# A delta rule whose decay rows are read from HBM with a broadcast, and whose decay factors form during the step ahead

## What is computed

```
g = cumsum(g)                                      # per head, over the chunk
decay = exp(g[:, None] - g[None, :])               # where i >= j, else 0
L = strict_lower((beta*k) @ k.T * decay);  A = L + I
u, w = solve(A, v*beta), solve(A, k*beta*exp(g))
qk = (q @ k.T) * decay
v_new = u - w @ S
o = (q*exp(g)) @ S + qk @ v_new
S = S*exp(g_last) + (k*exp(g_last - g)).T @ v_new
```

## Time and profile before

| | us |
|---|---|
| median of 3 runs | 3170.73 |
| range of the runs | 3170.51 to 3170.89 |
| the profiled execution, its own time | 3172.82 |
| its span | 3171.0 |
| TensorE busy | 3027.9 |
| DVE, ACT, POOL busy | 1636.5, 963.3, 959.6 |
| mean granted TensorE clock | 0.987 of full |

### The profile page before, as it was taken

One profiled execution on the slowest core, in us unless ns is written; L12 is line 12 of the kernel. 1 busy time (PEld: TensorE's weight loads), 2 busy tenths in 40 slices (PEclk: granted clock), 3 DMA queues, 4 the chain that ended last, 5 costly groups with the idle time before them and its releaser, 6 DMA issues.

```text
span 3171.0 us, 45836 instructions
## 1 busy us (share of the span) xinstructions
PE 3027.9 (95%) x19048; PEld 2834.2 (89%) x19048; DVE 1636.5 (52%) x2465; ACT 963.3 (30%) x1661; POOL 959.6 (30%) x497
## 2 busy tenths in 40 slices
PE   7999999999988887899999999999999999999997
PEld 6999999999878885699899999989999887798996
DVE  6556666884555555466767776212212348531223
ACT  3212212443522226532121223212112337532222
POOL 0333333323321210233333333232222222344442
PEclk9999999999999998999999999999999999999998
DMA  5434444224300012233433432121211210122221
GB/s 198 143 118 135 126 138 133 99 69 139 110 19 1 1 41 65 72 102 125 134 124 128 146 121 86 61 67 60 61 61 60 78 47 2 61 94 93 94 92 62
DMA packets 124444, 282.63 MB, mean 89 GB/s; under 512 B 40014, under 2 KB 57166, under 8 KB 123982
## 3 DMA queue, kind: packets, MB, share of 16 engines
q1 hardware_dynamic: 121358, 272.24, 26.9%
q10 hardware_dynamic: 2880, 7.45, 0.6%
HBM read 268.08 MB, written 15.08 MB: 89 GB/s over the span
## 4 chain that ended last, share of the span: by engine, by line
PE 86%; DVE 6%; ACT 4%; issue 2%; POOL 1%; DMA 1%; ACTq 0%; SPq 0%; DVEq 0%; POOLq 0%
PE psum L1658 76%; PE psum L1796 2%; PE psum L1788 2%; PE psum L1895 1%; DVE o_acc L1483 1%; PE psum L1883 1%; ACT prob_o L1175 1%; DVE prob_o L1595 1%; PE psum L1876 1%; PE psum L1836 1%; PE psum L1802 0%; ACT cacc L1022 0%; ACT dE L1141 0%; DVE ada_w L1376 0%; PE psum L1825 0%
## 5 line engine op out<-in xcount | busy, mean ns | idle before, releaser
L829 POOL TENSOR_TENSOR wl<-raw,wh 128x1024 fp32r<-128x1024 f32 (+1 forms) x326 | 831.4, 2550 | 1712.2 <-ACT wh L907 1711.0
L1658 PE MATMUL psum<-uh,wh 128*128 128x256 f32 (+5 forms) x2704 | 661.7, 326 | 21.2 <-DVE ul L1230 11.2
L1658 PE MATMUL psum<-uh,wl 128*128 128x256 f32 (+5 forms) x2704 | 660.7, 326 | 0.0
L1658 PE MATMUL psum<-ul,wh 128*128 128x256 f32 (+5 forms) x2704 | 660.7, 325 | 0.0
L1658 PE MATMUL psum<-ah,wh 128*128 128x386 f32 (+4 forms) x2192 | 595.7, 344 | 5.5 <-POOL wl L829 4.4
L1658 PE MATMUL psum<-ah,wl 128*128 128x386 f32 (+4 forms) x2192 | 591.2, 342 | 0.0
L1658 PE MATMUL psum<-al,wh 128*128 128x386 f32 (+4 forms) x2192 | 588.8, 341 | 0.0
L1658 PEld LDWEIGHTS psum<-uh,wh 128*128 128x128 f32 (+1 forms) x2704 | 452.3, 190 | 45.3 <-issue 23.8
L1376 DVE SCALAR_TENSOR_TENSOR ada_product<-ada_w,cb 128x1024 f32<-128x1024 f32 x256 | 478.2, 1868 | 5.1
L1658 PEld LDWEIGHTS psum<-uh,wl 128*128 128x128 f32 (+1 forms) x2704 | 452.5, 189 | 19.8
L1658 PEld LDWEIGHTS psum<-ul,wh 128*128 128x128 f32 (+1 forms) x2704 | 451.5, 190 | 19.9
(11 more groups left out here) (211 smaller groups left out, 2515.1 us busy)
## 6 DMA issues: line engine op xcount, KB each, us to landing
raw<-in_w SPq DMA_DIRECT2D x264, 512.0 KB, 3.6
ada_w<-in_ada_w SPq DMA_DIRECT2D x128, 512.0 KB, 3.9
raw<-in_w SPq DMA_DIRECT2D x64, 448.0 KB, 3.7
spill<-cacc ACTq DMA_DIRECT2D x16, 384.0 KB, 2.4
scale_w<-in_scale_w SPq DMA_DIRECT2D x8, 512.0 KB, 14.4
ada_start<-in_ada_w SPq DMA_DIRECT2D x8, 512.0 KB, 14.6
ada_w<-bias_final SPq DMA_DIRECT2D x16, 256.0 KB, 3.1
h<-in_xT SPq DMA_DIRECT2D x8, 384.0 KB, 14.3
```

The source lines that it names most:

```text
L829: nc.gpsimd.tensor_tensor(wl[n % SPLIT_SLOTS][:, 0:k * w], raw[n % RAW_SLOTS][:, 0:k * w], wh[n % SPLIT_SLOTS][:, 0:k * w].bitcast(f32), A ...
L1658: ins = nc.tensor.matmul(pair[0:w, lo:hi], wt[n % SPLIT_SLOTS][:, k * w:(k + 1) * w], xt[:, k, cols], start=first, stop=last)
```

## The change

A new item `("rows",)` follows the last projection. TensorE transposes the sums `gc` of all 48 combinations of chunk, direction and head into 48 rows of 128, DVE copies them to SBUF (into `dQS[0]`), and SP stores them in HBM (`rows_hbm`). For the steps 1 to 5 SP then reads the four rows of a direction straight into `dE`, each into all 128 partitions: for step 1 as soon as they are stored, for step st + 2 after `dnU` of step st. Those steps have no products of the gates any more. DVE's subtraction now reads `dE` in SBUF and stands in the step ahead, behind `dnN` of level 4 (direction 0) and of level 5 (direction 1); ACT's two functions stand behind `dnY` of the same levels. POOL's queue is as it was. Step 0 is formed as before. Branches for norms that are not late, which this program never takes, are deleted as well, so line numbers move.

```diff
+    s += [("rows",)]
...
+            def load_rows(st, d):
+                first = 8 * SCAN[d][st] + 4 * d
+                sp.dma_start(dE[2 * (st % 2) + d][:, :, :], rows_hbm[first:first + 4, :].unsqueeze(0).to_broadcast([P, 4, P])) \
+                    .then_inc(rows_loaded[d], 16)
...
+                if x == ("rows",):
+                    sp.wait_ge(rows_ready, 1)
+                    sp.dma_start(rows_hbm, gc_rows[0:STEPS * 8, :]).then_inc(rows_stored, 16)
+                    sp.wait_ge(rows_stored, 16)
+                    sp.wait_ge(product_done, number[("proj", 0, "nv", 3)] + 1)
+                    for d in range(2):
+                        load_rows(1, d)
+                if x[0] == "dnU" and x[1] + 2 < STEPS:
+                    sp.wait_ge(product_done, number[x] + 1)
+                    sp.wait_ge(dif_done, group(x) + 3)
+                    load_rows(x[1] + 2, x[2])
...
+            def decay_factor(st, d):                       # ACT
+                n, b = 2 * st + d, 2 * (st % 2) + d
+                act.wait_ge(dif_done, n + 1)
+                nc.scalar.activation(dE[b][:, :, :], dE[b][:, :, :], ACT.Abs).then_inc(abs_done, 1)
+                act.wait_ge(abs_done, n + 1)
+                nc.scalar.activation(dE[b][:, :, :], dE[b][:, :, :], ACT.Exp, scale=-1.0).then_inc(decay_ready, 1)
...
-                elif x[0] == "dnA":
...
+                elif x[0] == "dnA" and x[1] == 0:
+                    decay_factor(0, x[2])
...
+                if x[0] == "dnY" and x[2] == 1 and x[1] < LAST and x[3] in (4, 5):
+                    decay_factor(x[1] + 1, x[3] - 4)
...
+            def decay_difference(st, d):                   # DVE
+                b = 2 * (st % 2) + d
+                dve.wait_ge(rows_loaded[d], 16 * st)
+                nc.vector.tensor_tensor(dE[b][:, :, :], dE[b][:, :, :], per_head(gc, SCAN[d][st], d), ALU.subtract).then_inc(dif_done, 1)
...
+                elif x[0] == "rows":                       # DVE
+                    dve.wait_ge(product_done, i + 1)
+                    nc.vector.tensor_copy(gc_rows[0:STEPS * 8, :], banks_of(x)[0:STEPS * 8, 0:P]).then_inc(rows_ready, 1)
...
+                if x[0] == "dnN" and x[2] == 1 and x[1] < LAST and x[3] in (4, 5):
+                    decay_difference(x[1] + 1, x[3] - 4)
...
+                elif x[0] == "rows":                       # PE
+                    pe.wait_ge(cum_scaled, 1)
+                    nc.tensor.transpose(pair[0:STEPS * 8, 0:P], gc[:, :, :].rearrange("p t c -> p (t c)"), ident[:, :]) \
+                        .then_inc(product_done, 1)
...
-                    for hd in range(4):
+                    for hd in range(0 if x[1] else 4):
                         c = 4 * d + hd
                         nc.tensor.matmul(pair4(pair, 0)[:, hd, :], decay[:, tile, c:c + 1].to_broadcast([P, P]), masks[:, U[d], :],
```

More of the change, by code:

```diff
@@ L224, in build @@
     late_no = {m: i for i, m in enumerate(LATE_NORMS)}
-    early_no = {x[1]: i for i, x in enumerate([x for x in norm_items if x[1] not in late_no])}
     norm_of = lambda x: 3 * x[1] + 2 * x[2] if x[0] in ("gate", "up", "down") else 3 * x[1] + 1
@@ L340, in build @@
         scratch = nc.dram_tensor("spill", (16, P, T), f32, kind="Internal").ap()
+        gc_rows = dQS[0][:, 0, :]
+        rows_hbm = nc.dram_tensor("rows_hbm", (STEPS * 8, P), f32, kind="Internal").ap()
         toeplitz = nc.dram_tensor("toeplitz", (16, NA_HEADS, 15, 48), f32, kind="Internal").ap()
@@ L362, in build @@
         squared, sq_summed, std_ready, rstd_ready = sem("squared"), sem("sq_summed"), sem("std_ready"), sem("rstd_ready")
-        normed, u_hi, u_lo = sem("normed"), sem("u_hi"), [sem(f"u_lo{i}") for i in range(2)]
         silu_done, glu_done, a_hi, a_lo = sem("silu_done"), sem("glu_done"), sem("a_hi"), sem("a_lo")
@@ L376, in build @@
         z_loaded = [sem(f"z_loaded{j}") for j in range(len(zt))]
+        rows_ready, rows_stored, rows_loaded = sem("rows_ready"), sem("rows_stored"), [sem(f"rows_loaded{d}") for d in range(2)]
         masks_loaded, table_made, bias_made, nv_loaded, nqk_loaded, m8_loaded, rope_loaded = (sem(n) for n in
@@ L421, in released @@
                 return [(cum_read, 2)]
+            if kind == "rows":
+                return [(rows_ready, 1)]
             if kind == "dnT":
                 return [(at_ready, n), (qk_ready, n)]
-            return [({"norm": std_ready, "gate": silu_done, "up": glu_done, "l2": l2_std,
+            return [({"norm": std_ready, "l2": l2_std,
                       "cum": cum_read, "dnA": lmat_done, "dnN": n_ready, "dnY": y_ready, "dnX": x_ready, "dnV": kd_ready,
@@ L629, in build @@
         dny_split_at = {("S", j): j for j in range(STEPS)}
[L631 to L643, removed]
         def mod_terms(x, *terms):
@@ L1091, in _ @@
                             finish_product(y)
[L1092 to L1099, removed]
                 elif x in scaled_no:
@@ L1104, in _ @@
                         gates()
[L1105 to L1116, removed]
                 elif x[0] == "l2":
@@ L1352, in a_matrix @@
                 d, n, tile, b = x[2], group(x), SCAN[x[2]][x[1]], work(x)
+                dve.wait_ge(product_done, number[x] + 1)
                 dve.wait_ge(em_ready, n + 1)
@@ L1433, in _ @@
                             finish_product(y)
[L1434 to L1456, removed]
+                    for k in range(KD if x == final else 0):
+                        if k >= 2:
+                            dve.wait_ge(out_stored[k % 2], 16 * (k // 2))
+                        nc.vector.scalar_tensor_tensor(out=sq[k % 2][:, 0:last], in0=h[:, k, 0:last],
+                                                       scalar=norm_g[:, 3 * DEPTH, k:k + 1], in1=rstd[:, u_cols(0, last)],
+                                                       op0=ALU.mult, op1=ALU.mult).then_inc(out_ready, 1)
                 elif x in scaled_no:
@@ L1461, in _ @@
                         gates()
[L1462 to L1473, removed]
                 elif x[0] == "abt":
@@ L1495, in _ @@
                                                    op0=ALU.mult, op1=ALU.mult).then_inc(cum_read, 1)
+                elif x[0] == "rows":
+                    dve.wait_ge(product_done, i + 1)
+                    nc.vector.tensor_copy(gc_rows[0:STEPS * 8, :], banks_of(x)[0:STEPS * 8, 0:P]).then_inc(rows_ready, 1)
                 elif x[0] == "dnA":
                     d, n, tile, b = x[2], group(x), SCAN[x[2]][x[1]], work(x)
-                    dve.wait_ge(product_done, i + 1)
-                    nc.vector.tensor_tensor(dE[b][:, :, :], pair4(banks_of(x), 0), per_head(gc, tile, d),
-                                            ALU.subtract).then_inc(dif_done, 1)
+                    if x[1] == 0:
+                        dve.wait_ge(product_done, i + 1)
+                        nc.vector.tensor_tensor(dE[b][:, :, :], pair4(banks_of(x), 0), per_head(gc, tile, d),
+                                                ALU.subtract).then_inc(dif_done, 1)
                     if d == 1:
@@ L1728, in _ @@
                         fresh_norm[0] = m
-                        if m in late_no:
-                            pe.wait_ge(shift_lo, KD + late_no[m])
-                            ready = lambda k: pe.wait_ge(late_lo, KD * late_no[m] + k + 1)
-                        else:
-                            ready = lambda k: pe.wait_ge(u_lo[k % 2], KD // 2 * early_no[m] + k // 2 + 1)
+                        pe.wait_ge(shift_lo, KD + late_no[m])
+                        ready = lambda k: pe.wait_ge(late_lo, KD * late_no[m] + k + 1)
                     if x[0] == "down" and x[4] == 0:
```

1 line of the change is left out of this document (removed).

## The result

The changed kernel takes 3148.57 us (median of 4 runs, 3146.39 to 3152.17), the kernel before 3170.62 (4 runs, 3164.04 to 3170.89): a ratio of 0.9936, 95% interval 0.9920 to 0.9952. Forecast were 3149.5 us and a range of 3145 to 3158. The profiled execution took 3149.65, its span is 3147.9, 23.1 less than before.

A forecast was written before the change was run, and what follows sets the result against it. TensorE was taken as the bound, with the decay factor's relay in the transitions. 14.8 + 5.4 - 0.3 + 1.3 = 21.2 off 3172.82 gives 3151.6; the profile stands 2.1 above the median, so 3149.5; range 3145 to 3158.

The forecast's parts named there:

- What bounds the kernel: TensorE, busy 3027.9 of 3171.0 us; its waits are above all in the delta rule's five transitions between steps.
- The relay: In each transition, the decay factor's way through DVE, ACT, ACT, POOL ahead of `a_matrix`; said to go.
- the rival in which a new wait eats half: DVE and POOL meet again, each transition gives only TensorE's 1.79 us: 9.0 in all, 3161.7 us; chance 0.10.
- What goes: Transitions lose 16 TensorE instructions (1.79 us) and the relay: 3.7 us each, 14.8 for four; POOL becomes the bound.
- The first transition: From step 0 to 1, with `dnU` in place of `dnK`: 5.4 us earlier.
- What is added: Subtractions (0.69), ACT's functions and POOL's masks inside the levels fit in idle time: cost nothing.
- The rival of disturbed levels: POOL's 20 moved masks each hold up DVE by 1.12 us, 22.4 come back: 3171.9 us, no change; chance 0.05.
- The start: TensorE's first products of `dnA` wait for DVE's copy of the rows: 0.3 us lost, bounds 0 and 1.6.
- The transfer: A 256 KB load of rows takes 4.1 us by the nearest row, within more than 15 us of slack: costs nothing.
- The rival of late rows: Loads of rows take 48 us, some 28 too late, in four steps 112: 3261 us, slower; chance 0.05.
- The clock: Two transitions lose 1.29 us each to clock falls after TensorE's 1.85 us hole; one fall saved, 1.3 us.
- TensorE's busy time: Sign of being right: TensorE is 8.9 us less busy.

The follow-up runs named there:

- The experiment without the early part: Changed kernel with subtraction, absolute value and exponential back at dnA of their own step, products of the gates still gone: 3170.88 us, ratio 1.0001 to the kernel before.
- its own experiment: Changed kernel with POOL's four masks of dnT reordered, A of both directions first, then the two transposes: 3144.98 us, ratio 0.9924 to the kernel before.
- the experiment with other banks: Changed kernel with the transposed rows in other PSUM banks, those of the item cum: 3150.75 us, ratio 0.9931 to the kernel before.

## Why the prediction was right, point by point

- *What bounds the kernel.* Right. The relay and TensorE's products run side by side in a transition. The experiment without the early part gives the time of before, with the products gone. The rival in which a new wait eats half falls: POOL's three masks stayed at 1.27 or 1.28 us and the additions took 0.69 and 0.83, so the two engines hardly met.
- *What goes.* Right in every link that sets the length of the transition. Forecast from `dnV`: POOL's mask of A of direction 1 ends after 11.85, measured 11.81; DVE's second mask after 13.15, measured 13.12; `dnX` after 15.85, measured 15.93. Off the path, level 1 of direction 0 started after 9.99 in place of 10.25. The first transition: the second mask after 11.35, measured 11.34; 5.4 shorter forecast, 5.58 measured at `dnX` (18.82 to 13.24). Without the clock the five came to 20.2 forecast; measured 22.77 less the two falls before (1.30 and 1.31) is 20.16. That POOL is the new bound was confirmed by its own experiment. There, I expected 1.2 us in the four transitions and 1.4 in the first, and got 1.07 and 1.08. No row of that run shows TensorE waiting in front of level 1, so what bounds the transition next is open.
- *What is added.* Right as to nothing, with one detail off. The subtraction took 0.78 on average in place of 0.69: five of the ten run beside POOL's mask and take 0.88. They have two inputs in SBUF, the masks and copies of the levels have one input in PSUM and stayed at 0.69. That is what the Trainium skill says on the page "SBUF — State Buffer", section "SBUF: two separate sides", and the trace agrees. The rival of disturbed levels falls: no mask or copy of the levels took over 0.69. The row that the prediction holds against it doesn't bear on it, though: DVE's mask at 1044.62 starts after POOL's work ends at 1044.54. The mask before it does, at 1043.65, with 0.69 as well.
- *The start.* 0.3 forecast, 0.17 measured (45.12 to 45.29, and the experiment with other banks gives it back).
- *The transfer.* 4.1 from the nearest row, 3.2 measured. The rival of late rows falls: nothing waited. By the Trainium skill, page "DMA: Bandwidth & Descriptors", section "Anatomy of one DMA — SWDGE (gpsimd) path", it would be 2.6, an estimate. That section is about transfers that GpSimd issues, and these are issued by SP; the measurement decides.
- *The clock.* The sum is right by luck, the picture only by half. I took one fall saved of two, 1.3 us, as the middle between none and both. Both transitions lost theirs (2.61), and a new one came in level 4 of step 5 (1.44), after a longer hole that the kernel before had too: 1.17 net.
- *TensorE's busy time.* Wrong: 8.9 us less was forecast, 14.3 it is, 12.6 of it inside the delta rule (277.8 to 265.3, from DVE's last scaling to the first transpose of o). Steps 3 and 4, without a fall of the clock before or after, lost 2.17 and 2.25 us each where 1.79 was forecast. Busy time counts an instruction at a lower clock at its longer duration, so the net of one fall less is in the sum. What makes the other 0.4 us per step isn't shown; eight instructions in front of a stop count 1.06 us where they take 0.89 in a row, and TensorE stops less often now.
- *The spread.* I took the runs of before as tight (0.4 us). Over 13 runs of one chip they spread over 11 us. The forecast of 3149.5 hit 3148.57 closer than such runs allow one to claim; what carries the explanation are the steps within the profiles, which repeat to 0.05 us between the two profiles of the changed kernel.

## What to carry to other kernels

Two paths that run side by side have to be shortened together: here the products alone brought 0.27 us of 3.64, the early factors alone 1.86. Work that depends on nothing in the step belongs into the holes of the step ahead, and on VectorE a hole can be read off as the idle time in front of the instruction that follows. Write the new relay out link by link with the durations of the old timeline: here it named the next bound, and reordering that engine was the next experiment.

## What the runs showed of the hardware

- A DMA that reads the same 2 KB for each of 128 partitions (256 KB) landed in 3.2 us, a plain load of the same size in 2.9 to 4.5.
- With six otherwise useless products in a hole of 2.36 us, TensorE's granted clock was 1.00 over the following 6 us in the one profile taken, where it was 0.72 without them, and the step was 1.44 us shorter.
- VectorE's operation with two inputs in SBUF waits for GpSimd's (0.69 becomes 0.83 or 0.88, 1.81 in the old transition, and it ends 0.55 us after GpSimd's each time), one with an input in PSUM doesn't (0.69 in either case). GpSimd's mask that starts during such an operation waits as well (1.27 becomes 1.72 or 1.80).
